# RWKV preparation: the next pair of heads projected beside the present pair's chain, no GpSimd arithmetic, reciprocal root by logarithm and exponential

## Chip, cores and metric

One NeuronCore of a Trainium2 chip runs the whole program. The metric is device time in microseconds; the kernel before takes 3918.95 us (median of three runs, 3918.48 to 3922.56). Engines are named as in the profile: PE (matrix products; PEld its weight loads), DVE, ACT, POOL, and SP, which issues DMAs.

## What is computed

Two transformer blocks, one behind the other. The change lies in the second block's RWKV-7 mixer, 8 heads of 64 channels over 1024 positions, both directions in time. In the reference's terms (T = 1024, float32):

```
u = h @ w_in; u_rwkv = u + mu_prev * (prev - u) + mu_next * (next - u)
r, k, v, g_lo, wf_lo, wb_lo, af_lo, ab_lo = split(u_rwkv)
kk = k * k_k per head; kk = kk / max(sqrt(sum(kk * kk)), 1e-12)
decay = exp(-exp(-0.5) * sigmoid(w0 + tanh(w_lo) @ w_up));  a = sigmoid(a0 + a_lo @ a_up)
k_d = k * (1 + (a_d - 1) * k_a)                    # d: forward, backward
S = S * decay - (S kk) (a kk)^T + v k_d^T;  y = S r      # scan over time, both directions
bonus = sum over head((k_f + k_b) * r * r_k) * v;  out = (groupnorm(y_f + y_b) + bonus) * g
```

Around it stand attention, output projections and a mixture of experts, which the change doesn't touch.

## The kernel before

The program is a row of stages. A stage is a block with an instruction list for each engine and its own semaphores; all engines meet at its end. Engines execute their list in order, so a wait holds up everything behind it on that engine.

Channels lie on partitions and time along the free dimension; a pair of heads is 128 channels. `stage_rwkv_low` (L1715 on) projects three blocks of 128 columns, 12 to 14 of the RWKV part: the low-rank inputs of gate, decay and rate. Each block is 48 products: 8 slices of the depth, two halves of time, and three fp32r products for one in float32 (`split_product`; `high_part` on ACT, `low_part` on DVE make the two halves of a weight, in two slots). `shifted` (L1688 on) turns a projected block into its token-shifted form: ACT copies it from PSUM with a scale (L1697), DVE adds the previous (L1701) and the next position (L1705). SP loads the weights and writes hT, the stage's input of 4 MB, to DRAM (L1740). POOL sets up `scan_reset`.

`rwkv_pairs` loops over the four pairs of heads (hardware loop `Fori`, register `pr`) with three stages:

- `stage_rwkv_prepare` (L1803 on), called the preparation below. PE projects k, r and v of this pair in float32 (L1853; a float32 product shows as two records, so a projection of 16 products is 32) and sums squares over each head (L1860). DVE and ACT turn that into the normalised key: maximum (L1925), root (L1893), reciprocal (L1927), product (L1929). Four products (L1871) make the inputs of decay and rate for both directions, ACT takes their sigmoids (L1896, L1899). DVE scans the decay within chunks of 64 positions (L1935); POOL subtracts the decay of the position itself (L1915) and multiplies rate by key (L1918); ACT takes three exponentials a direction (L1905, L1907, L1909); DVE makes the keys (L1939, L1942), the bonus' dot products (L1945, L1947, summed over heads by PE at L1877) and the four operands of the chunk stage (L1952 to L1961, `chunk_operands`).
- `stage_rwkv_chunks`: the scan in chunks of 64, some 3240 small products on PE.
- `stage_rwkv_out`: group norm, bonus and gate into `yrT[:, pr]`. SP also reads hT back, because the chunk stage's tiles overwrite it.

What is read and written where in PSUM: `bank2(n)` is two banks, 1024 columns. PE projects into `bank2` 1, 0 and 2, the norm goes to 3, decay and rate to 3, 0, 1 and 2 again. The order of the work is that of the lists and the `wait_ge` calls; nothing is planned by a program.

## Time and profile before

| | us |
|---|---|
| median of three runs | 3918.95 |
| profiled execution | 3924.63 |
| its span, first to last instruction | 3922.8 |
| low-rank stage | 46.6 |
| one pair: preparation, chunks, out | some 85, 132, 15 |
| all four pairs, 1852.9 to 2780.9 | 928 |

Engine shares of the span: PE 81%, DVE 55%, ACT 34%, POOL 11%. The profile is one execution on the chip. A row of the timeline gives the start, the duration, engine, line, operation, the tile written and the tile read, shapes and count, and in brackets how long the engine was idle before it and who ended that. PEclk is the granted clock of PE as a share of full speed: 0.5 is 1.2 GHz and 1.00 is 2.4 GHz.

### The profile page before, as it was taken

Reading aid. Unit: us, or ns where it says so; the run is one execution under the profiler, and the core shown is the slowest. Engines: PE = TensorE matmul, PEld = TensorE weight load, DVE = VectorE, ACT = ScalarE, POOL = GpSimd, SP = SyncE. Lnnn points to the kernel's source line nnn. Section 1 sums busy time; section 2 is a strip of 40 time slices with the busy share of each in tenths; the row PEclk is TensorE's granted clock in tenths of the full one; section 3 lists DMA queues with packets and bytes.
Section 4 is the critical chain, followed back from the end, with each engine's and each line's share of the span. In section 5 each row is a group of like instructions: output and inputs, shape, how many; then the busy total and the mean of one; then the engine's idle time right before and its main releaser. Section 6 shows DMA issues by size and latency. Waiting matters only on the chain. (4 is left out here: it accounts for less than half of the span.)

```text
span 3922.8 us, 58296 instructions
## 1 busy us (share of the span) xinstructions
PE 3194.4 (81%) x24517; PEld 2476.0 (63%) x24517; DVE 2172.2 (55%) x2577; ACT 1343.7 (34%) x1777; POOL 423.9 (11%) x256
## 2 busy tenths in 40 slices
PE   6699957589999898777686876769699982999995
PEld 1478745478888676654382754638466671888884
DVE  7632254456666333363674747657311238888885
ACT  1321143312121222354242423324210121777774
POOL 0200011300000010211121202112000000121210
PEclk8699977789999999898797887879799985999997
DMA  8131103111111322102001010100311224999996
GB/s 330 47 92 46 30 1 113 59 54 49 48 49 36 140 85 98 43 17 77 1 4 61 3 63 1 46 18 4 114 33 37 108 108 151 359 399 398 396 396 214
DMA packets 219994, 424.20 MB, mean 108 GB/s; under 512 B 13120, under 2 KB 122642, under 8 KB 219538
## 3 DMA queue, kind: packets, MB, share of 16 engines
q1 hardware_dynamic: 212434, 394.75, 28.1%
q0 software_dynamic: 4608, 16.78, 1.7%
q10 hardware_dynamic: 2753, 9.66, 0.6%
q8 instruction: 168, 2.75, 0.3%
q14 instruction: 31, 0.25, 0.0%
HBM read 387.61 MB, written 33.55 MB: 107 GB/s over the span
## 5 line engine op out<-in xcount | busy, mean ns | idle before, releaser
L213 DVE TENSOR_TENSOR w_exp_low<-w_exp,w_exp_high 128x2048 fp32r<-128x2048 f32 x192 | 438.0, 2291 | 56.6 <-ACT w_exp_high L208 56.5
L208 ACT ACTIVATE w_exp_high<-w_exp 128x2048 fp32r<-128x2048 f32 x192 | 367.9, 1919 | 126.2 <-PE psum L221 126.2
L219 PE MATMUL psum<-ffn_high,w_high 128*128 128x512 f32 x704 | 274.7, 390 | 9.0 <-DVE w_low L213 9.0
L220 PE MATMUL psum<-ffn_low,w_high 128*128 128x512 f32 x704 | 274.6, 390 | 0.0
L221 PE MATMUL psum<-ffn_high,w_low 128*128 128x512 f32 x704 | 274.4, 390 | 0.0
L1375 DVE SCALAR_TENSOR_TENSOR ffn_hidden<-u_padded,param_columns,ffn_hidden 128x1024 f32 (+1 forms) x176 | 226.2, 1285 | 23.8 <-DVE ffn_hidden L1375 0.2
L219 PE MATMUL psum<-w_exp_high,x_turned_high 128*128 128x512 f32 x512 | 204.0, 398 | 7.0 <-DVE w_exp_low L213 7.0
L1853 PE MATMUL psum<-mixers_hT,w_rkv 128*128 128x512 f32 x384 | 176.6, 622 | 37.7 <-DMA w_rkv<-in_w_in 37.7
L221 PE MATMUL psum<-w_exp_high,x_turned_low 128*128 128x512 f32 x512 | 201.3, 393 | 0.0
L220 PE MATMUL psum<-w_exp_low,x_turned_high 128*128 128x512 f32 x512 | 200.9, 392 | 0.0
L2288 DVE COPY inverse<-psum 64x512 f32<-64x512 f32 x192 | 121.8, 637 | 74.3 <-PE psum L2123 48.9
L1853 PEld LDWEIGHTS psum<-mixers_hT,w_rkv 128*128 128x128 f32 x384 | 76.5, 201 | 135.4 <-issue 96.1
L219 PE MATMUL psum<-ffn_down_w_split,ffn_down_lhs_split 128*128 128x512 f32 x352 | 140.4, 399 | 22.8 <-DVE ffn_down_lhs_split L213 17.2
L219 PEld LDWEIGHTS psum<-ffn_high,w_high 128*128 128x128 f32 x704 | 132.6, 188 | 36.8 <-DVE w_low L213 9.4
L2222 ACT ACTIVATE inverse<-psum 64x512 f32<-64x512 f32 x192 | 106.9, 557 | 131.7 <-PE psum L2123 105.8
L221 PEld LDWEIGHTS psum<-ffn_high,w_low 128*128 128x128 f32 x704 | 132.6, 188 | 27.6
L220 PEld LDWEIGHTS psum<-ffn_low,w_high 128*128 128x128 f32 x704 | 132.6, 188 | 27.5
L2557 DVE TENSOR_TENSOR gates_sb<-gates_sb,psum 128x1024 f32<-128x1024 f32 x16 | 19.5, 1221 | 232.7 <-PE psum L2505 232.7
L513 PE MATMUL psum<-masks,norm_h 128*128 128x128 f32 x272 | 60.2, 397 | 102.3 <-POOL norm_h L502 63.9
L213 DVE TENSOR_TENSOR ffn_down_w_split<-ffn_down_ring,ffn_down_w_split 128x1024 fp32r<-128x1024 f32 x44 | 53.9, 1225 | 158.1 <-ACT ffn_down_lhs_split L208 158.1
L220 PE MATMUL psum<-ffn_down_w_split,ffn_down_lhs_split 128*128 128x512 f32 x352 | 139.5, 396 | 0.0
L221 PE MATMUL psum<-ffn_down_w_split,ffn_down_lhs_split 128*128 128x512 f32 x352 | 139.5, 396 | 0.0
(435 smaller groups left out, 7822.3 us busy)
## 6 DMA issues: line engine op xcount, KB each, us to landing
w_exp<-in_exp_w_gate SPq DMA_DIRECT2D x32, 2048.0 KB, 11.3
w_exp<-in_exp_w_up SPq DMA_DIRECT2D x32, 2048.0 KB, 11.1
w_exp<-in_exp_w_down SPq DMA_DIRECT2D x32, 2048.0 KB, 11.4
...
```

Of the source, the lines that this page charges most:

```text
L208: return nc.scalar.activation(out, src, ACT.Copy, scale=scale)
L213: return nc.vector.tensor_tensor(out, src, high.bitcast(F32), ALU.subtract)
L219: nc.tensor.matmul(out, left[0], right[0], start=start, stop=False)
L220: nc.tensor.matmul(out, left[0], right[1], start=False, stop=False)
L221: return nc.tensor.matmul(out, left[1], right[0], start=False, stop=stop)
L513: ins = nc.tensor.transpose(ps[:, 2 * (t % 4) + k // 4, (k % 4) * P:(k % 4 + 1) * P], hbuf[:, t % SLOTS, k * P:(k + 1) * P], core.mask(M_ID))
L1375: ins = nc.vector.scalar_tensor_tensor(out=out, in0=src, scalar=weight, in1=out, op0=ALU.mult, op1=ALU.add)
L1853: ins = nc.tensor.matmul(ps[:, 2 * m + h, :], w[n][:, kt], hT[:, kt, 512 * h:512 * h + 512], start=(kt == 0), stop=(kt == KD - 1))
L2222: nc.scalar.activation(place[rows[1], :], ps[rows[1], inverse_bank(n, 1), columns], ACT.Copy).then_inc(inv_lower[n % 2], 1)
L2288: nc.vector.tensor_copy(place[rows[0], :], ps[rows[0], inverse_bank(n, 0), columns]).then_inc(inv_upper[n % 2], 1)
L2557: nc.vector.tensor_tensor(sg[:, h], sg[:, h], ps[:, 4 * h + 2:4 * h + 4, :], ALU.mult).then_inc(parts, 1)
```

## The change

- k, r and v of a pair are no longer projected in its own preparation. The first pair's are three more blocks (columns 4, 0 and 8 of 128) of the low-rank stage, six in all, with split products; the tiles `next_k`, `next_r` and `next_v` (the last quarter of `yrT`) keep them. The preparation of pair p projects those of pair p + 1 into `bank2` 1, 2 and 3 (float32 as before), if there is a next pair (`more`).
- On PE the order is now: norm, decay and rate products, projection of k and r, sums over heads for the bonus, projection of v. The shifts of all three stand at the end of ACT's and DVE's lists.
- `stage_rwkv_low`: weights in three slots used twice; the sigmoid and tanh of the low-rank inputs stand between the blocks.
- The root and reciprocal are the exponential of -0.5 times the logarithm, both on ACT.
- POOL's four operations a preparation are gone: rate by key goes to DVE; the difference and its exponential are replaced by a product of the key with the decay of the neighbouring position, a shifted read within each chunk of 64, and a copy of the key at the chunk's edge. POOL sets up `scan_reset` in each preparation, since its old place is taken.
- One exponential tile for each direction instead of one for both; v is copied out by ACT.
- The loop runs three times; the fourth pair follows as straight code without projection.

```diff
-    reset = core.reset = core.at("scan_reset", 140, [P, 2, T])
+    core.next_k = core.at("next_k_cm", 140, [P, T])
...
+    core.next_v = core.yrT[:, 3, :]
     w = [core.at(f"w_low{n}", 28 + 4 * n, [P, KD, P]) for n in range(3)]
-    split = core.at("w_low_split", 108, [P, 2, 2, KD, P], F32R)
+    split = core.at("w_low_split", 148, [P, 2, 2, KD, P], F32R)
+    blocks = [(12, low[:, 0]), (13, low[:, 1]), (14, low[:, 2]), (4, core.next_k[:]), (0, core.next_r[:]), (8, core.next_v)]
+    NB = len(blocks)
...
+        parts = [shifted(dst, flat[:, 1024 * (n % 4):1024 * (n % 4) + T], core, block, nc.scalar, nc.vector,
+                         got, half, shift, n) for n, (block, dst) in enumerate(blocks)]
...
+            for n, (block, _) in enumerate(blocks):
+                if n >= 3:
+                    sp.wait_ge(low_done, n - 2)
+                sp.dma_start(w[n % 3][:], weight_columns(dram["w_in_2"][0], block * P, P)).then_inc(w_in[n % 3], 16)
+                if n == 2:
+                    sp.dma_start(hT_in_dram(core), hT[:]).then_inc(hT_out, 16)
...
+            for n in range(NB):
                 pe.wait_ge(low_done, n + 1)
+                if n >= 4:
+                    pe.wait_ge(shift, n - 3)
...
-            for n in range(2):
-                act.wait_ge(shift, n + 1)
-                nc.scalar.activation(low[:, n], low[:, n], funcs[n]).then_inc(act_done, 1)
+                if n in (3, 4):
+                    act.wait_ge(shift, n - 2)
+                    nc.scalar.activation(low[:, n - 3], low[:, n - 3], funcs[n - 3]).then_inc(act_done, 1)
...
-            parts[0][1]()
-            take(2)
-            parts[1][1]()
-            parts[2][1]()
-
...
-        @s.b.gpsimd
-        def _(pool):
-            nc.gpsimd.memset(reset[:], 1.0).then_inc(ones_done, 1)
...
+            for n in range(NB):
+                if n + 2 < NB:
+                    take(n + 2)
+                parts[n][1]()
+
+
+def stage_rwkv_prepare(core, hT, pr, more):
...
+    k, r = core.next_k, core.next_r
+    reset = core.at("scan_reset", 44, [P, 2, T])
+    kk = core.at("kk_cm", 52, [P, T])
...
+    e = [core.at(f"growth{d}", kb, [P, T]) for d, kb in enumerate((200, 196))]
...
+    NORM, W_UP, A_UP, DOTS, NEXT = 0, (1, 2), (3, 0), 0, (1, 2, 3)
...
+        follow = ((1, k[:]), (0, r[:]), (2, core.next_v)) if more else ()
+        parts = [shifted(dst, bank2(NEXT[n]), core, pr + (4 * m + 1), nc.scalar, nc.vector, got, half, shift, n)
+                 for n, (m, dst) in enumerate(follow)]
...
+            for n, (m, _) in enumerate(follow):
+                sp.dma_start(w[n][:], weight_columns(dram["w_in_2"][0], pr * P + (m * RD + P), P)).then_inc(w_in[n], 16)
+
+        @s.b.gpsimd
+        def _(pool):
+            nc.gpsimd.memset(reset[:], 1.0).then_inc(reset_done, 1)
+            pool.wait_ge(reset_done, 1)
+            for d, first in enumerate((0, RCH - 1)):
+                nc.gpsimd.memset(chunks(reset[:, d])[:, :, first:first + 1], 0.0).then_inc(reset_done, 1)
...
+            def project(n):
...
-                        ins = nc.tensor.matmul(ps[:, 2 * m + h, :], w[n][:, kt], hT[:, kt, 512 * h:512 * h + 512],
+                        ins = nc.tensor.matmul(ps[:, 2 * NEXT[n] + h, :], w[n][:, kt], hT[:, kt, 512 * h:512 * h + 512],
...
+            pe.wait_ge(sq_done, 1)
+            over_heads(NORM).then_inc(norm_mm, 1)
...
-                ins.then_inc((w_mm, a_mm)[m], 1)
+            for d in range(2):
+                ups(0, d, W_UP[d]).then_inc(w_mm, 1)
+            ups(1, 0, A_UP[0]).then_inc(a_mm, 1)
+            pe.wait_ge(norm_cut, 1)
+            ups(1, 1, A_UP[1]).then_inc(a_mm, 1)
+            if more:
+                pe.wait_ge(sg_done, 1)
+                project(0)
+                pe.wait_ge(sg_done, 2)
+                project(1)
...
-            ins.then_inc(dots_mm, 1)
+            pe.wait_ge(a_done, 2)
+            over_heads(DOTS).then_inc(dots_mm, 1)
+            if more:
+                project(2)
...
+            nc.scalar.activation(t1[:], k[:], ACT.Square, scale=col("k_k_2")).then_inc(sq_done, 1)
+            nc.scalar.activation(vc[:], core.next_v, ACT.Copy).then_inc(v_kept, 1)
...
+            for d in range(2):
                 act.wait_ge(w_mm, d + 1)
-                nc.scalar.activation(sg[d][:], bank2(first), ACT.Sigmoid, bias=col(names["w0"][d])).then_inc(sg_done, 1)
-            for d, first in enumerate((1, 2)):
+                nc.scalar.activation(sg[d][:], bank2(W_UP[d]), ACT.Sigmoid, bias=col(("w0_f_2", "w0_b_2")[d])
+                                     ).then_inc(sg_done, 1)
+            for d in range(2):
                 act.wait_ge(a_mm, d + 1)
-                nc.scalar.activation(a[d][:], bank2(first), ACT.Sigmoid, bias=col(names["a0"][d])).then_inc(a_done, 1)
+                nc.scalar.activation(a[d][:], bank2(A_UP[d]), ACT.Sigmoid, bias=col(("a0_f_2", "a0_b_2")[d])
+                                     ).then_inc(a_done, 1)
+            act.wait_ge(norm_cut, 1)
+            nc.scalar.activation(kk[:], kk[:], ACT.Ln).then_inc(log_done, 1)
+            act.wait_ge(log_done, 1)
+            nc.scalar.activation(kk[:], kk[:], ACT.Exp, scale=-0.5).then_inc(root_done, 1)
...
             for d in range(2):
-
-                act.wait_ge(diff_done, d + 1)
-                if d:
-                    act.wait_ge(m_used, 1)
-                nc.scalar.activation(e[:], src[:, d, 0], ACT.Exp, scale=-DECAY_SCALE).then_inc(bar_exp, 1)
                 act.wait_ge(scan_done, d + 1)
                 nc.scalar.activation(src[:, d, 1], b[d][:], ACT.Exp, scale=-DECAY_SCALE).then_inc(p_exp, 1)
-                act.wait_ge(bar_used, d + 1)
-                nc.scalar.activation(e[:], b[d][:], ACT.Exp, scale=DECAY_SCALE).then_inc(m_exp, 1)
-
-        @s.b.gpsimd
-        def _(pool):
-            for d in range(2):
-                pool.wait_ge(scan_done, d + 1)
-                nc.gpsimd.tensor_tensor(src[:, d, 0], b[d][:], sg[d][:], ALU.subtract).then_inc(diff_done, 1)
-                pool.wait_ge(kk_done, 1)
-                pool.wait_ge(a_done, d + 1)
-                nc.gpsimd.tensor_tensor(src[:, d, 3], a[d][:], kk[:], ALU.mult).then_inc(akk_done, 1)
+                nc.scalar.activation(e[d][:], b[d][:], ACT.Exp, scale=DECAY_SCALE).then_inc(m_exp, 1)
+            for n in range(len(parts)):
+                act.wait_ge(rkv_mm, n + 1)
+                if n == 0:
+                    act.wait_ge(kk_done, 1)
+                    act.wait_ge(kd_done, 2)
+                if n == 1:
+                    act.wait_ge(dots_in, 1)
+                    act.wait_ge(p_used, 2)
+                if n == 2:
+                    act.wait_ge(v_kept, 1)
+                parts[n][0]()
...
 
         @s.b.vector
         def _(dve):
-            parts[0][1]()
-            parts[1][1]()
             dve.wait_ge(norm_mm, 1)
-            nc.vector.tensor_scalar(kk[:], bank2(3), 1e-24, None, ALU.max).then_inc(norm_cut, 1)
-            dve.wait_ge(norm_root, 1)
-            nc.vector.reciprocal(kk[:], kk[:]).then_inc(norm_inv, 1)
-            dve.wait_ge(norm_inv, 1)
-            nc.vector.scalar_tensor_tensor(out=kk[:], in0=k[:], scalar=col("k_k_2"), in1=kk[:], op0=ALU.mult,
-                                           op1=ALU.mult).then_inc(kk_done, 1)
-            parts[2][1]()
+            nc.vector.tensor_scalar(kk[:], bank2(NORM), 1e-24, None, ALU.max).then_inc(norm_cut, 1)
             for d in range(2):
                 dve.wait_ge(sg_done, d + 1)
                 way = slice(None) if d == 0 else slice(None, None, -1)
-                nc.vector.tensor_tensor_scan(b[d][:, way], core.reset[:, d, way], sg[d][:, way], 0.0,
+                if d == 0:
+                    dve.wait_ge(reset_done, 3)
+                nc.vector.tensor_tensor_scan(b[d][:, way], reset[:, d, way], sg[d][:, way], 0.0,
                                              ALU.mult, ALU.add).then_inc(scan_done, 1)
...
             dve.wait_ge(kd_done, 2)
+            dve.wait_ge(norm_mm, 1)
             nc.vector.tensor_tensor(t1[:], src[:, 0, 2], src[:, 1, 2], ALU.add).then_inc(sum_kd, 1)
             dve.wait_ge(sum_kd, 1)
             nc.vector.scalar_tensor_tensor(out=t1[:], in0=t1[:], scalar=col("r_k_2"), in1=r[:], op0=ALU.mult,
                                            op1=ALU.mult).then_inc(dots_in, 1)
+            dve.wait_ge(root_done, 1)
+            nc.vector.scalar_tensor_tensor(out=kk[:], in0=k[:], scalar=col("k_k_2"), in1=kk[:], op0=ALU.mult,
+                                           op1=ALU.mult).then_inc(kk_done, 1)
+            dve.wait_ge(kk_done, 1)
             for d in range(2):
-                dve.wait_ge(bar_exp, d + 1)
-                dve.wait_ge(kk_done, 1)
-                nc.vector.tensor_tensor(src[:, d, 0], kk[:], e[:], ALU.mult).then_inc(bar_used, 1)
+                nc.vector.tensor_tensor(src[:, d, 3], a[d][:], kk[:], ALU.mult).then_inc(akk_done, 1)
                 dve.wait_ge(p_exp, d + 1)
+                bar, decay, key = chunks(src[:, d, 0]), chunks(src[:, d, 1]), chunks(kk[:])
+                here, before, edge = ((slice(1, RCH), slice(0, RCH - 1), slice(0, 1)) if d == 0 else
+                                      (slice(0, RCH - 1), slice(1, RCH), slice(RCH - 1, RCH)))
+                nc.vector.tensor_tensor(bar[:, :, here], key[:, :, here], decay[:, :, before], ALU.mult)
+                nc.vector.tensor_copy(bar[:, :, edge], key[:, :, edge]).then_inc(bar_done, 1)
                 end = RCH - 1 if d == 0 else 0
-                nc.vector.tensor_copy(pl[:, d], src[:, d, 1].rearrange("p (c t) -> p c t", t=RCH)[:, :, end]
-                                      ).then_inc(pl_done, 1)
+                nc.vector.tensor_copy(pl[:, d], decay[:, :, end]).then_inc(pl_done, 1)
+                dve.wait_ge(bar_done, d + 1)
                 dve.wait_ge(pl_done, d + 1)
                 nc.vector.tensor_tensor(src[:, d, 1], src[:, d, 1], r[:], ALU.mult).then_inc(p_used, 1)
                 dve.wait_ge(m_exp, d + 1)
                 dve.wait_ge(akk_done, d + 1)
-                nc.vector.tensor_tensor(src[:, d, 2:4], src[:, d, 2:4], e.ap().unsqueeze(1).to_broadcast([P, 2, T]),
+                nc.vector.tensor_tensor(src[:, d, 2:4], src[:, d, 2:4], e[d].ap().unsqueeze(1).to_broadcast([P, 2, T]),
                                         ALU.mult).then_inc(m_used, 1)
-                if d == 0:
-                    dve.wait_ge(dots_mm, 1)
-                    nc.vector.tensor_tensor(bonus[:], bank2(0), vc[:], ALU.mult).then_inc(bonus_done, 1)
+            dve.wait_ge(v_kept, 1)
+            dve.wait_ge(dots_mm, 1)
+            nc.vector.tensor_tensor(bonus[:], bank2(DOTS), vc[:], ALU.mult).then_inc(bonus_done, 1)
+            for n in range(len(parts)):
+                parts[n][1]()
...
@@ -2430,10 +2443,13 @@
 
 
 def rwkv_pairs(core, hT):
-    with core.nc.Fori(0, RH // 2) as pr:
-        stage_rwkv_prepare(core, hT, pr)
+    with core.nc.Fori(0, RH // 2 - 1) as pr:
+        stage_rwkv_prepare(core, hT, pr, True)
         stage_rwkv_chunks(core)
         stage_rwkv_out(core, hT, pr)
+    stage_rwkv_prepare(core, hT, RH // 2 - 1, False)
+    stage_rwkv_chunks(core)
+    stage_rwkv_out(core, hT, RH // 2 - 1)
 
 
 
```

## Rows read from the trace of the kernel before

A window's row gives its stretch and length, then busy us and instructions of PE, PEld, DVE, ACT and POOL, PE's granted clock, and the DMA engines' share and GB/s.

**Rows 1.** The page's first part: engine, busy us (share of the span), instructions.
```profile
PE 3194.4 (81%) x24517; PEld 2476.0 (63%) x24517; DVE 2172.2 (55%) x2577; ACT 1343.7 (34%) x1777; POOL 423.9 (11%) x256
```

**Rows 2.** Busy time by stage: low-rank, chunks 1, preparation 2, chunks 2; columns as above.
```profile
1806.00:1852.60 46.60, 35.63 (x144) 28.94 (x144) 11.61 (x12) 9.69 (x9) 1.98 (x3) 0.89 0.35 124
...
1937.20:2069.10 131.90, 110.70 (x3240) 102.06 (x3240) 89.70 (x223) 53.32 (x121) 25.82 (x18) 0.89 0.01 3
...
2084.00:2169.50 85.50, 55.24 (x120) 23.23 (x120) 46.11 (x26) 20.92 (x19) 13.02 (x4) 0.80 0.08 21
2169.50:2301.50 132.00, 111.07 (x3240) 102.14 (x3240) 89.48 (x223) 53.26 (x121) 25.82 (x18) 0.89 0.01 3
```

**Rows 3.** Line view: first of a preparation, first of DVE in the chunk stage.
```profile
L1883 ACT ACT_TABLE_LOAD  x4: 1283/1283/1283, 1852.9 to 2549.3; - x4
...
L2275 DVE MEMSET pair_states<- x4: 165/165/165, 1937.5 to 2634.4; 128x128 f32 x4
```

**Rows 4.** Timeline, preparation of the second pair: ACT and PE.
```profile
2084.33 1.28 ACT L1883 ACT_TABLE_LOAD   x1 [3.29 <-PEq L185]
...
2089.26 30.41 PE L1853 MATMUL psum<-mixers_hT,w_rkv 128*128 128x512 f32 x64 [9.61 <-DMA w_rkv<-in_w_in]
...
2110.19 1.15 ACT L1890 ACTIVATE temp<-k_cm,param_columns 128x1024 f32<-128x1024 f32 x1 [3.00 <-DVE k_cm L1705]
...
2121.22 13.90 PE L1853 MATMUL psum<-mixers_hT,w_rkv 128*128 128x512 f32 x32
...
2135.05 3.70 PE L1871 MATMUL psum<-rwkv_low,w_ups 64*128 64x512 f32 x12
...
2138.43 2.12 ACT L1896 ACTIVATE decay_sigmoid<-psum,param_columns 128x1024 f32<-128x1024 f32 x2
...
2158.80 3.78 PE L1877 MATMUL psum<-temp,masks 128*128 128x512 f32 x4 [17.55 <-DVE temp L1947]
```

**Rows 5.** Timeline of the same preparation: DVE.
```profile
2123.76 1.22 DVE L1925 TENSOR_SCALAR kk_cm<-psum 128x1024 f32<-128x1024 f32 x1
...
2126.10 6.55 DVE L1927 RECIPROCAL kk_cm<-kk_cm 128x1024 f32<-128x1024 f32 x1 [1.12 <-ACT kk_cm L1893]
...
2139.58 4.47 DVE L1935 TENSOR_TENSOR_SCAN decay_sum<-scan_reset,decay_sigmoid 128x1024 f32<-128x1024 f32 x2 [0.36 <-ACT decay_sigmoid L1896]
...
2157.46 1.28 DVE L1947 SCALAR_TENSOR_TENSOR temp<-temp,param_columns,r_cm 128x1024 f32<-128x1024 f32 x1
...
2164.62 1.23 DVE L1952 TENSOR_TENSOR chunk_operands<-kk_cm,decay_exp 128x1024 f32<-128x1024 f32 x1
2165.76 0.17 DVE L1955 COPY pair_chunk_decay<-chunk_operands 128x16 f32<-128x16 f32 x1
...
2167.10 2.28 DVE L1961 TENSOR_TENSOR chunk_operands<-chunk_operands,decay_exp 128x2048 f32<-128x2048 f32 x1
...
2169.76 0.17 DVE L2275 MEMSET pair_states<- 128x128 f32 x1 [0.38 <-PEq L185]
```

**Rows 6.** Timeline, low-rank stage, ACT behind the first and the third block.
```profile
1826.41 1.06 ACT L208 ACTIVATE w_low_split<-w_low 128x1024 fp32r<-128x1024 f32 x1 [13.51 <-PE psum L221]
...
1848.09 1.11 ACT L1697 ACTIVATE rwkv_low<-psum,shift_keep 128x1024 f32<-128x1024 f32 x1 [9.76 <-PE psum L221]
```

**Rows 7.** Line view of L1844, the w_ups loads: from issue to landing.
```profile
DMA to landing us min/median/max: 2.5/3.4/5.6
```

**Rows 8.** Busy times of one microsecond, second pair; PEclk behind POOL's columns.
```profile
2094.00:2095.00 1.00, 1.00 (x2) 0.29 (x2) 0.00 (x0) 0.00 (x0) 0.00 (x0) 0.66 0.00 0
```

**Rows 9.** Timeline of the same preparation: POOL and DVE side by side.
```profile
2148.91 3.31 POOL L1915 TENSOR_TENSOR chunk_operands<-decay_sum,decay_sigmoid 128x1024 f32<-128x1024 f32 x1
2149.95 2.82 DVE L1939 TENSOR_SCALAR chunk_operands<-rate,param_columns,one_minus_ka 128x1024 f32<-128x1024 f32 x1
2152.19 2.78 POOL L1918 TENSOR_TENSOR chunk_operands<-rate,kk_cm 128x1024 f32<-128x1024 f32 x1
2152.81 3.24 DVE L1942 TENSOR_TENSOR chunk_operands<-chunk_operands,k_cm 128x1024 f32<-128x1024 f32 x1
```

93 lines of the change are left out of this document (29 added, 64 removed).

## Prediction, made before the change had run

> **What bounds the kernel now.** I read the page first, then the busy times by stage, then the preparation of the second pair of heads instruction by instruction. The page says that PE is busy 81% of the span [rows 1]; that is a mean over stages with different limits and says nothing of this change. The table by stage says more [rows 2]. The low-rank stage takes 46.6 us, the second pair's preparation 85.5, the chunk stage 131.9 in the first pair and 132.0 in the second. From ACT's first table load in a preparation to DVE's first instruction in the chunk stage it is 84.6 us in the first pair and 85.1 in the last [rows 3], 85.4 in the second. In a preparation PE is busy 55 of 85 us, DVE 46, ACT 21, POOL 13: no engine fills it, they take turns.
>
> The turns, in the second pair, which starts at 2084.33 [rows 4]: PE waits for weights until 2089.26, then projects k and r with the norm product behind them and v from 2121.22 on. DVE has nothing to work on but k's and r's shift and the key's norm until v is projected: the decay and rate products come at 2135.05. From there the chain is one of ACT, DVE and POOL, with PE idle but for the sums over heads at 2158.80 (3.78 us): sigmoids, scans, then DVE beside POOL, and the last product ends at 2167.10 + 2.28 = 2169.38 [rows 4, 5]. So a preparation is some 50 us of PE, then 35 us of DVE, one behind the other. The change makes them run beside each other.
>
> **1. The low-rank stage takes three more blocks.** Each is 48 split products. Blocks two and three there lie between the ACT instructions at 1826.41 and 1848.09, each of which waited for the end of a block [rows 6]: 21.68 / 2 = 10.84 us a block, 32.5 for three. The weight splitting (one ACT and one DVE instruction on 128x1024, by that shape 1.1 and 1.2 us, a block) falls into the block before, with two slots, and needs 2.5 us of 10.84. The last three weight loads are queued on SP behind the 4 MB copy of hT; the first of them is wanted two blocks after its issue (over 20 us). Nothing of this shows. The bank set that block 4 takes over was read by DVE three blocks earlier. Behind the last block, the ACT and DVE instructions of its shift take 1.11 + 2 x 1.28 as before. What ends the stage now is ACT with 1.11, a table load of 1.28 and two activations of the sigmoids' shape (2.12 for two [rows 4]), 4.5; these move forward into the blocks, 3.8 stays: 0.7 back. **Cost 31.8 us**; at worst 36 (a weight load late by half a block).
>
> **2. Pairs 1 to 3: what is left of a preparation.** I count from ACT's table load (S, 2084.33 in the second pair). Table load 1.28 and the square of k, 1.15, end at S+2.5 [rows 4]. The norm product (4 records) is the first work of PE behind an idle stretch, so it takes what the cold sum over heads took: 3.78, to S+6.4. DVE's cut of the norm: 1.22, to S+7.7 [rows 5]. The four w_ups loads are now issued first; each lands 2.5 to 5.6 us from its issue [rows 7], the last issue at about S+2.5, so PE has them at S+5.5 to S+8. Take S+6.4. The decay products of both directions run in one another's shadow (12 records took 3.70 us where one by one would be 12 x 0.43 = 5.2 [rows 4]); eight of them count as four. The clock: in the second pair PE began at 2089.26 and the granted clock rose from 0.5 (1.2 GHz) to 1.0 (2.4 GHz) within the stretch 2094 to 2095, whose mean is 0.66 [rows 8], 5.4 us later. By that it rises at S+8: two steps of 0.85, two of 0.43, decays ready at S+9.1; the rate products one step of four behind, S+10.7. The first sigmoid (2.12 for two, [rows 4]) frees the bank for the projection at S+10.3. So PE begins to project at S+10.7.
>
> From there PE is the bound: three projections of 32 records, 13.90 us each [rows 4] (0.43 a record), with the sums over heads, 4 records, now warm, 1.7: 3 x 13.8 + 1.7 = 43.1, to S+53.8. Then ACT 1.11, DVE 2 x 1.28 and some 0.2 between them for v: S+57.7, and 0.4 to the chunk stage as now (2169.38 to 2169.76): 58.1. For a later rise of the clock and the wait for w_ups I add 1.2: **59.3**. Bounds: 57 if the rise comes earlier; 63 if the norm and all the step products run at 0.85 and the first 3 us of projection too.
>
> Is DVE done by then? Scans 4.47 from S+10.4; two pairs of rate instructions (below), 4.0; sum, dot and key 3 x 1.3 [rows 5]; then, for each direction, three products of 1.23 (rate by key, the shifted decay, r), one of 2.28 and two copies of 0.17, with gaps 6.5. That is 10.4 + 4.5 + 4.0 + 3.9 + 13.0 = S+35.8. The bonus waits for the sums over heads (S+40), then k's and r's shift follow by S+47, while PE still projects v until S+54. So DVE has 7 us to spare, the reciprocal of 6.55 [rows 5] is gone from its list, and the logarithm and exponential lie on ACT, which is busy under 25 us. The memset of scan_reset on POOL, now in every preparation, has until S+10.4 for some 2 us. The gain over three pairs, 84.6, 85.4 and 85.1 less 59.3 each, is 255.1 - 177.9 = **77.2 us** (66 to 84).
>
> **3. The last pair** has no projection. DVE's list above then sets the end: S+35.8 and the bonus 1.23, with 0.4 to the next stage and 0.4 for gaps: 37.8. Gain 85.1 - 37.8 = **47.3**. One term of it is unseen: the rate instructions. They take 2.82 and 3.24 us now, but beside POOL. The second DVE product started at 2152.81, POOL's ended at 2152.19 + 2.78 = 2154.97, and DVE's ended at 2156.05: 1.08 us after POOL [rows 9]. The first, at 2149.95, ended 0.55 after POOL's 2152.22. So each seems to stand still until POOL is done, and takes 0.6 and 1.2 alone; the four then take 4.0 with gaps instead of 2 x (2.82 + 3.24) = 12.1. If the durations were their own, the last pair would be 8.1 longer (the looping pairs have 7 us of that to spare). I take the short ones.
>
> The Trainium skill (SBUF — State Buffer, § Terms) states what these rows only suggest: DVE and GpSimd arbitrate for one port pair, "Lock-allocated, exclusive, held for the full instruction". By it the four instructions fall to 4.0 us and the sum stands; by the reading in which the long durations are DVE's own the sum is -84.6. By that page the new memset on POOL, which reads no SBUF, would hold up no product of two tensors.
>
> The shifted decay is a strided read of 16 x 63 elements, which no row of this stage shows; between one and two plain products. I take the plain product's 1.23; the other end costs 2.4 in the last pair and nothing in the others.
>
> **4. The loop.** Three iterations and a straight copy. If fetching new code cost time, the first iteration's chunk stage would be longer than the second's; it is 131.9 against 132.0 [rows 2]. I cost the copy at nothing, at most 3 us. The chunk and output stages are unchanged. The chunk stage's start could profit from a PE that stopped 4 us ago rather than 7: 0 to 2 us a pair, not taken.
>
> **Sum.** -77.2 - 47.3 + 31.8 = **-92.7 us**. The profiled execution takes 3924.6 (span 3922.8), the median of the runs 3918.95; a stage's length doesn't depend on which, so I take it from the median: 3826.
>
> **Rivals.**
> A. The overlap fails. PE executes in order and the projections stand ahead of the sums over heads, and behind waits on sigmoids; if they start only when DVE's chain is done (because of a wait that I misread), a preparation is 36 + 42 + 4 = 82 us, three pairs give 3 x 3, the last 47, less 32: -24, so 3895. For it: PE's queue is one list. Against: the waits in front of the projections name sigmoids that end at S+12 and nothing later. 5%. This is also the case in which the change doesn't do what it says.
> B. The clock. In the low stretch of small products and waits PE stays at 1.2 GHz longer, and part of the projection too: 5 us more in each of three pairs, and a slow last pair, or DVE's terms at their long ends: -92.7 + 15 + 8 = -70, so 3849. The cold 3.78 of a four-record product behind an idle stretch [rows 4] speaks for it, the rise within 5.4 us against. 15%. (The Trainium skill, TensorE: Matmul & The Clock Gate, § HAM oscillation — how this bites in real kernels, warns of kernels in which waits between groups of products throw the clock back each time; in the change's first 11 us there are four such waits, each short by my sum.)
> C. Slower than before: projections at 1.2 GHz throughout. A projection took 13.90 for 32 records at the high clock; at 0.85 a record 27.2, 13.4 more, for three projections in three pairs +120, and the time is 3946. It takes that the clock doesn't rise during 40 us of PE work without a gap; the tipping point is at 77% of the records at the low clock (92.7 / 120). Against it: in the same stage now the clock rose after 5.4 us and stayed. 2%.
> D. Better than the sum: an earlier rise, a warm start of the chunk stages: -105, 3814. 14%.
>
> **Chances.** Forecast (3820 to 3836) 64%, B 15% (3836 to 3860), D 14% (3805 to 3820), A 5%, C 2%. The range 3812 to 3848 takes in the forecast, half of B and more than half of D: some 80%. A measurement of this kernel tells 0.2% (8 us) from no change. Faster by more 0.97, within 0.01, slower 0.02.
>
> **What would show it.** In the trace of after: PE's projection starts 11 us behind ACT's first table load and runs to S+54 with no wait over 1 us; the last DVE instruction of the preparation is v's second shift; the rate instructions take 0.6 and 1.2; the last preparation is 38 long and DVE fills it from S+10 on; the low stage is 78 to 79 long. It is wrong if PE waits for the sums over heads, if the granted clock is 0.5 behind S+12, or if the last pair's DVE products keep 3.2 us.

## The result, and the profile after

The changed kernel takes 3821.89 us (median of four runs, 3814.73 to 3825.96), beside 3920.76 for the kernel before on the same chip: a ratio of 0.9745, 95% interval 0.9728 to 0.9762. The forecast was 3826, between 3812 and 3848. The profiled run is the one of 3825.96; its span is 3824.1.

I divide the region that the change touches, from the first load of the low-rank stage to the merge's first load, at the first load of each stage and at DVE's memset that opens the chunk stage. Microseconds, from the two traces:

| stage | before | after | difference | forecast |
|---|---|---|---|---|
| low-rank | 47.04 | 79.15 | +32.1 | +31.8 |
| preparations 1 to 3 | 84.48, 85.31, 84.93 | 58.49, 59.35, 57.92 | -79.0 | -77.2 |
| preparation 4 | 85.00 | 34.83 | -50.2 | -47.3 |
| chunks and output, four pairs | 588.1 | 588.7 | +0.6 | 0 |
| the region | 974.9 | 878.4 | -96.5 | -92.7 |

The spans differ by 98.7, so 2.3 us lie outside the region. The first part of the page of after, as in [rows 1]:

```profile
PE 3169.6 (83%) x24565; PEld 2477.3 (65%) x24565; DVE 2125.8 (56%) x2592; ACT 1340.5 (35%) x1776; POOL 381.6 (10%) x249
```

Its busy times by stage, low-rank, preparation 2, chunks 2 and preparation 4, with the columns of [rows 2]:

```profile
1807.00:1886.20 79.20, 68.16 (x288) 55.88 (x288) 22.72 (x21) 15.90 (x15) 0.00 (x0) 0.92 0.28 93
...
2090.00:2149.50 59.50, 51.78 (x121) 22.43 (x121) 33.82 (x29) 19.32 (x18) 1.98 (x3) 0.90 0.11 29
2149.50:2281.00 131.50, 111.70 (x3240) 102.74 (x3240) 88.94 (x221) 52.94 (x120) 25.81 (x18) 0.88 0.01 3
2503.10:2538.00 34.90, 11.06 (x24) 4.13 (x24) 26.21 (x23) 15.97 (x15) 1.98 (x3) 0.60 0.01 4
```

The page alone hides the change: PE's share went from 81 to 83%, and its busy time fell by only 25 us. The second preparation shows it. PE is busy 51.8 of 59.5 us where it was 55.2 of 85.5; DVE did 33.8 us of work in those same 59.5. In the last preparation DVE is busy 26.2 of 34.9.

The timeline of the second pair's preparation, ACT and PE; it starts (S) at 2090.07 and answers to [rows 4]:

```profile
2090.07 1.28 ACT L1898 ACT_TABLE_LOAD   x1 [3.27 <-PEq L185]
...
2093.30 3.78 PE L1858 MATMUL psum<-temp,masks 128*128 128x512 f32 x4 [7.88 <-ACT temp L1899]
2097.01 4.93 PE L1865 MATMUL psum<-rwkv_low,w_ups 64*128 64x512 f32 x16
...
2100.26 2.12 ACT L1903 ACTIVATE decay_sigmoid<-psum,param_columns 128x1024 f32<-128x1024 f32 x2 [6.80 <-PE psum L1865]
...
2101.87 27.73 PE L1873 MATMUL psum<-mixers_hT,w_rkv 128*128 128x512 f32 x64
...
2104.41 1.28 ACT L1910 ACT_TABLE_LOAD   x1
...
2106.78 1.28 ACT L1912 ACT_TABLE_LOAD   x1
...
2129.44 1.88 PE L1858 MATMUL psum<-temp,masks 128*128 128x512 f32 x4
...
2131.16 13.90 PE L1873 MATMUL psum<-mixers_hT,w_rkv 128*128 128x512 f32 x32
...
2145.19 1.11 ACT L1697 ACTIVATE rwkv_out_cm<-psum,shift_keep 128x1024 f32<-128x1024 f32 x1 [14.33 <-PE psum L1873]
```

From S+11.8 on PE has no gap to S+55.0. It never waits for DVE there: the sums over heads start in the record behind k's and r's projection. DVE in the same preparation, answering to [rows 5]:

```profile
2101.41 4.47 DVE L1938 TENSOR_TENSOR_SCAN decay_sum<-scan_reset,decay_sigmoid 128x1024 f32<-128x1024 f32 x2 [3.06 <-ACT decay_sigmoid L1903]
2105.80 0.79 DVE L1942 TENSOR_SCALAR chunk_operands<-rate,param_columns,one_minus_ka 128x1024 f32<-128x1024 f32 x1
2106.62 1.23 DVE L1945 TENSOR_TENSOR chunk_operands<-chunk_operands,next_k_cm 128x1024 f32<-128x1024 f32 x1
...
2114.90 1.20 DVE L1962 TENSOR_TENSOR chunk_operands<-kk_cm,chunk_operands 128x1008 f32<-128x1008 f32 x1
...
2123.47 2.28 DVE L1971 TENSOR_TENSOR chunk_operands<-chunk_operands,growth 128x2048 f32<-128x2048 f32 x1
2131.43 1.23 DVE L1975 TENSOR_TENSOR bonus<-psum,v_cm 128x1024 f32<-128x1024 f32 x1 [5.67 <-PE psum L1858]
...
2146.45 1.28 DVE L1701 SCALAR_TENSOR_TENSOR rwkv_out_cm<-psum,param_columns,rwkv_out_cm 128x1023 f32<-128x1023 f32 x1 [8.56 <-ACT rwkv_out_cm L1697]
2147.87 1.28 DVE L1705 SCALAR_TENSOR_TENSOR rwkv_out_cm<-psum,param_columns,rwkv_out_cm 128x1023 f32<-128x1023 f32 x1
2149.53 0.17 DVE L2288 MEMSET pair_states<- 128x128 f32 x1 [0.38 <-PEq L185]
```

The brackets are DVE's idle time: 5.67 us before the bonus and 8.56 before v's shift. The chain is done at 2125.75 (S+35.7) and waits for PE. The roles have changed places: PE's list sets the end, DVE has time to spare.

### The profile page after: what moved, and what is told of

It reads as the page before. It is cut to its first block and busy times, and to the rows that moved or that the text cites. A ratio compares the mean times of both kernels' runs of the same rounds, so it can differ in the third digit from the quotient of the medians.

```text
span 3824.1 us, 58374 instructions
## 1 busy us (share of the span) xinstructions
PE 3169.6 (83%) x24565; PEld 2477.3 (65%) x24565; DVE 2125.8 (56%) x2592; ACT 1340.5 (35%) x1776; POOL 381.6 (10%) x249
## 5 line engine op out<-in xcount | busy, mean ns | idle before, releaser
L1350 ACT ACTIVATE ffn_hidden<-ffn_hidden (+1 forms) x22 | 23.3, 1061 | 295.4 <-DVE ffn_hidden L1375 295.4
L219 PE MATMUL psum<-mix_out_w_split,mix_out_lhs_split 128*128 128x512 f32 x256 | 102.8, 402 | 27.7 <-DVE mix_out_lhs_split L213 20.9
## 6 DMA issues: line engine op xcount, KB each, us to landing
w_exp<-in_exp_w_up SPq DMA_DIRECT2D x32, 2048.0 KB, 10.4
```

The source lines that it names most:

```text
L219: nc.tensor.matmul(out, left[0], right[0], start=start, stop=False)
L1350: nc.scalar.activation(block(i * 2 + (j - 1)), block(i * 2 + (j - 1)), ACT.Silu).then_inc(silu_done, 1)
```

## Experiments

Whole times of one kernel lie within 11 us (after: 3814.73 to 3825.96), so a part worth less than 10 us is read from its stage, with the divisions of the table above. A "preparation" below is always such a length. It scatters too, by about 1 us, but only in its first part: from the projection's start to the chunk stage it is 47.66 us in each of the three looping preparations of after (2149.53 less 2101.87 in the second), and from the scans' start to the chunk stage 25.73 in the last (2538.11 less 2512.38). An edit behind these two points can be read from those lengths to a few hundredths. Diffs are against the changed kernel unless the text says otherwise, and are excerpts.

### The first half of the overlap taken away

```diff
-            if more:
-                pe.wait_ge(sg_done, 1)
-                project(0)
-                pe.wait_ge(sg_done, 2)
-                project(1)
...
-                project(2)
+                for n in range(3):
+                    project(n)
```

All three projections stand behind the sums over heads; everything else is as changed. DVE's list behind the dot products (the key, the operands, the bonus, 14 us) still runs beside them, so this takes away the overlap of the chain's first half only.

> The changed kernel, with all three projections of the next pair moved behind the sums over heads in PE's list, so behind DVE's dot products; the number of instructions is the same. Theory (the gain of pairs 1 to 3 is the overlap of PE's projections with the chain on ACT and DVE): in the changed kernel the dot products end 22.5 us behind a preparation's start and PE started to project at 11.8; now it idles, runs the sums over heads at the low clock (3.8), and starts to project at about 26, the first 5 us at the low clock. The preparation of pairs 1 to 3 grows from 59.5 to 74 or 75 us, the last pair's stays at 34.9, the whole is 45 us longer than the changed kernel. Rival (the gain comes from the shorter chain, and PE's order hardly matters): the preparation grows by less than 5 us.

Measured: 3862.01 us (3857.13 to 3870.72, four runs), ratio to before 0.9845 (0.9829 to 0.9861). Preparations 71.15, 72.41, 72.14 and 35.18; low-rank stage 79.26. PE in the second pair's preparation:

```profile
2132.62 3.78 PE L1858 MATMUL psum<-temp,masks 128*128 128x512 f32 x4 [10.64 <-DVE temp L1946]
2136.20 41.47 PE L1873 MATMUL psum<-mixers_hT,w_rkv 128*128 128x512 f32 x96
```

PE waits 10.64 us for DVE, takes 3.78 instead of 1.88 for the sums over heads, and then the three projections in one stretch. That costs 12.7 to 14.2 us in each of the first three preparations (39.9 in sum) and nothing in the last. So the order on PE is worth some 13 us a pair, and the last preparation's gain doesn't hang on it: there no projection is left at all. It is less than the 14.5 to 15.5 us a pair, 45 in all, that I expected: I had put the projection's first 5 us at the low clock, but the clock rose 3.8 us behind the start of the sums over heads, at about 2136.4, and 96 records took 41.47 us, 0.43 each.

### The chain alone

The kernel before, with its projections where they were, but the new chain: logarithm and exponential, the shifted product, rate by key on DVE, two exponential tiles, no POOL. (Diff against the kernel before, excerpts.)

```diff
-                    nc.scalar.activation(kk[:], kk[:], ACT.Sqrt).then_inc(norm_root, 1)
+                    nc.scalar.activation(kk[:], kk[:], ACT.Ln).then_inc(norm_root, 1)
+                    act.wait_ge(norm_root, 1)
+                    nc.scalar.activation(kk[:], kk[:], ACT.Exp, scale=-0.5).then_inc(norm_inv, 1)
...
-                nc.gpsimd.tensor_tensor(src[:, d, 0], b[d][:], sg[d][:], ALU.subtract).then_inc(diff_done, 1)
...
-            nc.vector.reciprocal(kk[:], kk[:]).then_inc(norm_inv, 1)
...
+                nc.vector.tensor_tensor(bar[:, :, here], key[:, :, here], decay[:, :, before], ALU.mult)
+                nc.vector.tensor_copy(bar[:, :, edge], key[:, :, edge]).then_inc(bar_used, 1)
```

> The kernel before, with only the edits of the chain: logarithm and exponential for root and reciprocal, rate by key on DVE, the shifted product in place of POOL's difference and its exponential. The projections stay where they were, the loop runs four times. Theory (what counts is the chain behind the projection of v, and the reciprocal was hidden behind that projection): DVE's list from the first scan to the last product took 29.8 us in the kernel before and 25.4 in the changed kernel's last pair, of which the key's product, 1.2, is done earlier here: 5.6 us less in each of four preparations, 22 us in all. Rival (each DVE instruction that goes is worth its own time): the reciprocal's 6.55 on top, 12 us a preparation and 48 in all.

Measured: 3898.69 us (3893.88 to 3902.68), ratio 0.9939 (0.9922 to 0.9955). Preparations 78.98, 79.37, 79.03, 79.14: 5.5, 5.9, 5.9 and 5.9 less than before. From PE and DVE of the second pair:

```profile
2119.70 13.90 PE L1854 MATMUL psum<-mixers_hT,w_rkv 128*128 128x512 f32 x32
...
2127.06 1.28 DVE L1915 SCALAR_TENSOR_TENSOR kk_cm<-k_cm,param_columns,kk_cm 128x1024 f32<-128x1024 f32 x1 [3.60 <-ACT kk_cm L1896]
...
2138.06 4.47 DVE L1921 TENSOR_TENSOR_SCAN decay_sum<-scan_reset,decay_sigmoid 128x1024 f32<-128x1024 f32 x2 [0.36 <-ACT decay_sigmoid L1899]
```

The key is ready at 2128.34, while v is projected until 2133.60 and the scans start only at 2138.06. The reciprocal of 6.55 us [rows 5] lay in that shadow before, so taking it away gains nothing here; the 5.8 come from the chain behind the scans.

### The old chain beside the overlap, whole and by one part

First the reciprocal alone (root, then DVE's reciprocal), then with it POOL's four operations and the exponential of the difference.

```diff
-            nc.scalar.activation(kk[:], kk[:], ACT.Ln).then_inc(log_done, 1)
-            act.wait_ge(log_done, 1)
-            nc.scalar.activation(kk[:], kk[:], ACT.Exp, scale=-0.5).then_inc(root_done, 1)
+            nc.scalar.activation(kk[:], kk[:], ACT.Sqrt).then_inc(root_done, 1)
...
+            nc.vector.reciprocal(kk[:], kk[:]).then_inc(log_done, 1)
+            dve.wait_ge(log_done, 1)
```

> The changed kernel with one part of the old chain: root on ACT and reciprocal on DVE instead of logarithm and exponential. Theory (as for the old chain): 6.5 us more in the last preparation, nothing in the first three, 6.5 in all. Rival (DVE sets the end everywhere): 26 us.

Measured: 3828.53 us (3820.82 to 3831.94), ratio 0.9767 (0.975 to 0.9783). Preparations 57.79, 59.9, 58.35 and 41.65: nothing in the first three beyond their scatter, 6.8 in the last. From the projection's start it is 47.66 in all three, as in after; from the last preparation's scans 32.33, 6.6 more. DVE has the 6.55 us to spare beside a projection and not without one.

The whole old chain adds to this (the two exponential tiles of the changed kernel stay):

```diff
+                nc.gpsimd.tensor_tensor(src[:, d, 0], b[d][:], sg[d][:], ALU.subtract).then_inc(diff_done, 1)
...
+                nc.gpsimd.tensor_tensor(src[:, d, 3], a[d][:], kk[:], ALU.mult).then_inc(akk_done, 1)
...
+                nc.scalar.activation(src[:, d, 0], src[:, d, 0], ACT.Exp, scale=-DECAY_SCALE).then_inc(bar_exp, 1)
...
-                nc.vector.tensor_tensor(src[:, d, 3], a[d][:], kk[:], ALU.mult).then_inc(akk_done, 1)
+                nc.vector.tensor_tensor(src[:, d, 0], src[:, d, 0], kk[:], ALU.mult).then_inc(bar_done, 1)
```

> The changed kernel with the old chain: root on ACT and reciprocal on DVE, and POOL's difference and rate by key back, with the difference's exponential on ACT. The projections stay beside the chain. Theory (PE sets the end in pairs 1 to 3, where DVE has 5.7 us idle ahead of the bonus and 8.6 ahead of v's shift; DVE sets it in the last pair): the last preparation grows by 6.6 for the reciprocal and by up to 10.4 for the stretches in which DVE stands still beside POOL, from 34.9 to 47 to 52; the first three by 0 to 3 each; 12 to 26 us in all. Rival (DVE's chain still sets the end in all four): 50 us or more.

Measured: 3841.84 us (3832.81 to 3846.28), ratio 0.9802 (0.9785 to 0.9818). Preparations 58.59, 58.34, 57.95 and 47.40: the last is 12.6 longer, the others are not; from the projection's start they are 47.66 or 47.67 again. POOL and DVE in the last one:

```profile
2507.30 7.00 POOL L1855 TENSOR_TENSOR chunk_operands<-decay_sum,decay_sigmoid 128x1024 f32<-128x1024 f32 x2 [9.32 <-DVE decay_sum L1945]
2509.32 2.77 DVE L1949 TENSOR_SCALAR chunk_operands<-rate,param_columns,one_minus_ka 128x1024 f32<-128x1024 f32 x1
2512.13 3.26 DVE L1952 TENSOR_TENSOR chunk_operands<-chunk_operands,next_k_cm 128x1024 f32<-128x1024 f32 x1
2515.31 0.80 DVE L1949 TENSOR_SCALAR chunk_operands<-rate,param_columns,one_minus_ka 128x1024 f32<-128x1024 f32 x1
2516.15 1.23 DVE L1952 TENSOR_TENSOR chunk_operands<-chunk_operands,next_k_cm 128x1024 f32<-128x1024 f32 x1
...
2527.82 5.67 POOL L1859 TENSOR_TENSOR chunk_operands<-rate,kk_cm 128x1024 f32<-128x1024 f32 x2 [13.51 <-DVE kk_cm L1962]
2528.91 2.31 DVE L1971 COPY pair_chunk_decay<-chunk_operands 128x16 f32<-128x16 f32 x1
```

The same two DVE instructions take 2.77 and 3.26 us beside POOL, and 0.80 and 1.23 once POOL has ended at 2514.30. Even the copy of 16 columns, 0.17 us elsewhere, takes 2.31. So of the chain's 23.2 us in the kernel before, 12.6 are left once PE sets the end of three preparations: the parts' gains overlap each other (the chain alone took 25.3 off the region, the overlap with the old chain 85.5, both 96.5).

### POOL's work put back without its dependences

These two settle whether the long durations come from POOL's being busy or from its reading SBUF. POOL works on the reset tile, which nobody needs any more, once the scans are done. First two products:

```diff
+            pool.wait_ge(scan_done, 2)
+            nc.gpsimd.tensor_tensor(reset[:, 0], reset[:, 0], reset[:, 1], ALU.mult).then_inc(reset_done, 1)
+            pool.wait_ge(reset_done, 4)
+            nc.gpsimd.tensor_tensor(reset[:, 0], reset[:, 0], reset[:, 1], ALU.mult).then_inc(reset_done, 1)
```

> The changed kernel with two POOL instructions that nobody waits for: products of two SBUF tensors of 128x1024, started when the second scan is done, as the first rate instruction is. Theory (a DVE instruction of this chain stands still while a POOL product runs; in the kernel before each ended 0.55 or 1.08 us behind POOL's): of the four rate instructions, 0.8 and 1.2 us long in the changed kernel, those beside POOL grow to the end of POOL's, 2 to 3.3 us; together 4 to 7 us more, in the last preparation at full size (35 becomes 39 to 42), in the others hidden in DVE's idle time. Rival (the 2.8 and 3.2 us of the kernel before were DVE's own, from the operands' places): the four keep 0.8 and 1.2.

Measured (one run, 3821.26): the last preparation 39.56 us, 4.7 longer, of which 4.1 lie behind the scans' start; the others 58.56, 59.39, 58.81. The last preparation:

```profile
2506.97 0.79 DVE L1946 TENSOR_SCALAR chunk_operands<-rate,param_columns,one_minus_ka 128x1024 f32<-128x1024 f32 x1
2507.13 2.83 POOL L1854 TENSOR_TENSOR scan_reset<-scan_reset 128x1024 f32<-128x1024 f32 x1 [11.96 <-DVE decay_sum L1942]
2507.79 3.25 DVE L1949 TENSOR_TENSOR chunk_operands<-chunk_operands,next_k_cm 128x1024 f32<-128x1024 f32 x1
2510.03 3.22 POOL L1856 TENSOR_TENSOR scan_reset<-scan_reset 128x1024 f32<-128x1024 f32 x1
2510.97 2.85 DVE L1946 TENSOR_SCALAR chunk_operands<-rate,param_columns,one_minus_ka 128x1024 f32<-128x1024 f32 x1
```

No data passes between the two engines, yet each DVE instruction that starts while POOL works ends 0.57 to 1.08 us after POOL (2511.04 against 2509.96, 2513.82 against 2513.25). Then three memsets of the same tile in the products' place:

```diff
+            nc.gpsimd.memset(reset[:], 1.0).then_inc(reset_done, 1)
```

> The same with three POOL memsets of 128x2048 (1.8 us each) in place of the products: they write SBUF and read nothing. Theory of one lock for every POOL instruction: rate instructions grow as beside the products, by up to 4 us in all. Rival (only a POOL instruction that reads SBUF holds up DVE's product of two tensors, while the single-tensor rate instruction may still be held up): the product keeps 1.2 us, the single-tensor one grows by up to 1.8.

Measured (one run, 3820.19): the last preparation 35.55, of which 26.04 lie behind the scans' start, 0.3 more than in after; the others 58.43, 59.12, 58.70.

```profile
2511.01 2.39 POOL L1854 MEMSET scan_reset<- 128x2048 f32 x1 [11.70 <-DVE decay_sum L1944]
2511.70 1.23 DVE L1951 TENSOR_TENSOR chunk_operands<-chunk_operands,next_k_cm 128x1024 f32<-128x1024 f32 x1
2512.84 1.11 DVE L1948 TENSOR_SCALAR chunk_operands<-rate,param_columns,one_minus_ka 128x1024 f32<-128x1024 f32 x1
2513.46 2.23 POOL L1856 MEMSET scan_reset<- 128x2048 f32 x1
...
2515.75 1.81 POOL L1858 MEMSET scan_reset<- 128x2048 f32 x1
```

The rival came out. The product of two tensors keeps its 1.23 beside a memset, and waits for a POOL product. The rate instruction that reads one tensor and columns is held up by both, here from 0.81 to 1.11, and it holds the memset up in turn: the two memsets that start while one runs take 2.39 and 2.23, the third, which meets only products of two tensors, 1.81. That a product of two tensors is held up only by a POOL instruction that reads SBUF is what the prediction took from the Trainium skill, SBUF — State Buffer (§ Terms, and § SBUF: two separate sides), and these two runs agree with it. For the sizes there is one run of each; the second and the last preparation of it agree.

### Where the first 11 us go

From S (in this and the next two sections SP's first load, 0.1 us behind ACT's first instruction in the second pair) to the projection nothing of PE's is hidden. Three edits shorten the ends of a looping preparation. The first moves the sigmoid's table load from the start of the preparation to the end of ACT's list in the stage before:

```diff
-            nc.scalar.preload_act_table(ACT.Sigmoid)
...
+            nc.scalar.preload_act_table(ACT.Sigmoid)
```

> The changed kernel with the sigmoid's table loaded at the end of ACT's list in the output stage, where ACT idles, rather than ahead of k's square. Theory (from a preparation's start to the norm product ACT is the path: table load 1.28, square 1.15): the norm product starts 1.9 rather than 3.2 us behind the start, and each of four preparations is 1.3 us shorter, 5 in all. Rival (the small w_ups loads take the place of the wait; by issue and landing they are there 5.0 to 5.6 us behind the start): the decay products start where they did, and the gain is under 0.5 us each.

Measured (one run, 3825.84): preparations 56.32, 59.47, 59.43, 34.60. The first is 2.2 shorter, the second and third are not, though ACT's square stands at the start of each. The square and the norm product, first and third pair:

```profile
1888.82 1.15 ACT L1898 ACTIVATE temp<-next_k_cm,param_columns 128x1024 f32<-128x1024 f32 x1 [3.16 <-PEq L185]
...
1890.02 3.78 PE L1858 MATMUL psum<-temp,masks 128*128 128x512 f32 x4 [5.51 <-ACT temp L1898]
...
2298.05 1.15 ACT L1898 ACTIVATE temp<-next_k_cm,param_columns 128x1024 f32<-128x1024 f32 x1 [2.07 <-PEq L185]
...
2301.65 3.78 PE L1858 MATMUL psum<-temp,masks 128*128 128x512 f32 x4 [8.37 <-issue]
```

In the first pair PE starts 1.20 us behind the square's start. In the third it starts 3.60 behind, 2.45 after the square has ended, and the trace names no engine that it waited for ("issue"). These are the preparations that are entered by the loop's jump back, and in them an instruction packet is moved:

```profile
q8 instruction: 1, 0.02, 0.9%
```

That is the DMA view from 2292 to 2302. PE seems to wait for its own instructions; the test is below. The last preparation isn't entered by the jump and its norm product does start 1.3 us earlier (S+1.2 for S+2.5), yet it is only 0.2 us shorter than after's: its granted clock rose at S+6.5, after's at S+5.6. In the first, 2.2 us shorter for a norm product 1.2 us earlier, the clock rose at S+5.0 instead of S+8.1.

The second edit shifts v in two halves, the first while PE projects the second:

```diff
+                    if n == 2 and h == 0:
+                        ins.then_inc(v_half, 1)
...
+                    for h, ready in enumerate(((v_half, 1), (rkv_mm, 3))):
+                        act.wait_ge(*ready)
+                        cols = slice(512 * h, 512 * h + 512)
+                        nc.scalar.activation(core.next_v[:, cols], bank2(NEXT[2])[:, cols], ACT.Copy,
+                                             scale=core.keep[:, bass.ds(pr + 9, 1)]).then_inc(got, 1)
...
```

> The changed kernel with the shift of v, last in pairs 1 to 3, taken in two halves of time, the first while PE projects the second half. Theory (behind PE's last product come ACT 1.11 and DVE 2 x 1.28 in full, 4.0 us): half the columns need 0.7 + 2 x 0.7 = 2.1, so 1.7 to 1.9 less in each of three preparations, 5 us in all; the last preparation is unchanged. Rival (PE's end isn't what the tail hangs on): no change.

Measured (one run, 3822.61): preparations 56.79, 56.11, 57.49, 35.22. The first three sum to 170.39, beside 175.76 in after: 5.4 less, with nothing in the last. In the second pair the chunk stage opens 2.67 us after v's last product instead of 4.47. Single preparations moved by 0.4 to 3.2, but from the projection's start each of the three is 45.86 us long instead of 47.66: 1.80 less each, as in the theory. The rest of the moves lies ahead of the projection.

### The changed kernel again, and one table for both functions

The changed kernel once more, as the measure for the next runs on that chip:

> The changed kernel itself, unedited, for its time on the chip on which the two below run. Expected: 97 us below the kernel before, from the stages of its first profile (low-rank +32, preparations -126, the rest even); both theories of the runs below take it as their zero.

Measured: 3823.62 us (3816.56 to 3830.47, five runs), ratio 0.9746 (0.9732 to 0.976); preparations 58.49, 59.20, 59.10, 35.78. A preparation repeats within 1.2 us. The next kernel names the set that holds logarithm and exponential:

```diff
+            nc.scalar.preload_act_table_set("natural_log_exp_and_others")
```

> The changed kernel with one table set that holds logarithm and exponential, loaded once, in place of two loads. Theory (ACT is not on the path there; in the last pair the exponential of the norm ended 3.2 us ahead of its use): one load of 1.28 us less on ACT in each preparation, all stages as long as before, within 0.3 us. Rival (ACT's exponentials set when DVE's products start): 1.3 us less in the last preparation.

Measured (one run, 3827.49): preparations 58.54, 59.48, 58.77, 35.18. ACT in the second:

```profile
2108.06 1.28 ACT L1909 ACT_TABLE_LOAD   x1
2109.35 1.06 ACT L1911 ACTIVATE kk_cm<-kk_cm 128x1024 f32<-128x1024 f32 x1
2110.44 1.06 ACT L1913 ACTIVATE kk_cm<-kk_cm 128x1024 f32<-128x1024 f32 x1
```

One load of 1.28 us has gone, and no stage is shorter by it: from the projection's start the first three are 47.66 or 47.67 as in after, and from the scans' start the last is 25.75, where it is 25.73 in after and 25.75 in its repetition. ACT isn't what ends any of them. (The Trainium skill, ScalarE: Activation LUTs, § Table sets: the hidden batching unit, has a logarithm and an exponential behind it share one load. In the trace of after they take two, L1910 and L1912; only with the set named is it one.)

### All three, and then no loop

> The changed kernel with the table load moved to the output stage, v's shift in halves, and one table set for logarithm and exponential. Theory (the parts lie one behind the other on the path of pairs 1 to 3): 3.1 us less in each of three preparations, 1.3 in the last, 10.5 us less than the changed kernel. Rival (one gives back what the other gains, at the w_ups loads or at DVE): 5 us or less.

Measured: 3810.17 us (3807.56 to 3817.3, five runs), ratio 0.971 (0.9697 to 0.9724). Preparations 54.47, 56.16, 57.64, 34.90, together 7.4 less than after and 9.4 less than its repetition. The halves of v's shift give their 1.80 in each of the first three (45.86 from the projection's start). It is short of the expected 10.5 where the table load's 1.3 us fails again: the norm product starts at S+3.1 in pairs 2 and 3, and at S+1.2 in pairs 1 and 4; and the fourth, at 34.90, isn't shorter than in after, since its clock rose 1.5 us later.

If PE waits there for instructions behind the jump, straight code takes the wait away:

```diff
-    with core.nc.Fori(0, RH // 2 - 1) as pr:
-        stage_rwkv_prepare(core, hT, pr, True)
+    for pr in range(RH // 2):
+        stage_rwkv_prepare(core, hT, pr, pr < RH // 2 - 1)
...
```

> The kernel with all three edits, with the four pairs written out as straight code instead of a hardware loop of three and a copy. With the table load moved, k's square ended 1.2 us behind a preparation's start in every pair, but PE's norm product stood at 1.2 only in pairs 1 and 4, and at 3.1 to 3.6 in pairs 2 and 3, which are entered by the loop's jump; a 16 KB instruction packet lies in the microsecond behind that start, and none in pair 4's. Theory (PE waits for its instructions behind the jump): in straight code the norm product starts at 1.2 in all four, preparations 2 and 3 are 2 us shorter, 4 us in all and no stage longer. Rival (it is the second and third pair's data, or the reload of hT): it stays at 3.1 to 3.6. Second rival (straight code is fetched more slowly): chunk stages longer than 132 us.

Measured: 3807.59 us (3802.22 to 3815.89, five runs), ratio 0.9709 (0.9696 to 0.9723). Preparations 54.59, 55.33, 54.63, 34.61. The second pair's norm product:

```profile
2080.83 1.15 ACT L1900 ACTIVATE temp<-next_k_cm,param_columns 128x1024 f32<-128x1024 f32 x1 [1.51 <-PEq L185]
...
2082.03 3.78 PE L1858 MATMUL psum<-temp,masks 128*128 128x512 f32 x4 [5.26 <-ACT temp L1900]
```

Its releaser is ACT again, at S+1.23, as in all four pairs, and no instruction packet is moved from 2072 to 2082. In both looping pairs it starts 1.9 us earlier than with the loop, which is what the theory said; the rival is out, and the second rival too, since chunk and output stages are 583.8 us together for 584.1. The second and third preparations are 3.8 us shorter together, and that this is 2 x 1.9 is partly luck: the second is 0.8 shorter and the third 3.0. One-microsecond rows, third pair, with the loop and without; PE's clock is the third number from the end:

```profile
2297.22:2298.22 1.00, 1.00 (x6) 0.36 (x6) 0.00 (x0) 0.00 (x0) 0.00 (x0) 0.84 0.82 197
...
2288.59:2289.59 1.00, 1.00 (x5) 0.53 (x6) 0.95 (x1) 0.00 (x0) 0.00 (x0) 0.91 1.15 345
```

By them PE's clock rose there at S+9.3 with the loop and at S+5.2 without; in the second pair it rose at S+6.3 and S+6.6. So an earlier norm product is shown, and what a stage gains by it depends on when the clock rises. The whole times of the last two kernels can't be told apart. Both beat the kernel before and the changed one: the region is 861.88 us long, beside 974.89 and 878.44.

## Why the prediction came out right

**The low-rank stage** was forecast at +31.8 and is +32.1. Blocks that differ only in their columns cost what their neighbours cost.

**Preparations 1 to 3.** Offsets from S in the second pair, forecast and measured:

| step | forecast | measured |
|---|---|---|
| norm product ends | 6.4 | 7.0 |
| scans start | 10.4 | 11.3 |
| projection starts | 10.7 | 11.8 |
| DVE's chain done | 35.8 | 35.7 |
| bonus starts | 40 | 41.4 |
| v projected | 53.8 | 55.0 |
| chunk stage | 58.1 + 1.2 | 59.5 |

The scans and the projection start a microsecond late, and PE's steps behind them keep their distance; DVE's chain took 24.3 us instead of 25.4 and made its delay good. In this pair the allowance of 1.2 for a later rise of the clock was needed: one-microsecond rows of this stretch, with PE's clock behind POOL's columns, have a clock of 0.85 between 2099 and 2100, so it rose at about 2099.3, 6.0 us from PE's start at 2093.30, where [rows 8] had it after 5.4. Over the three pairs most of it was not: the projection starts at S+10.8, 11.7 and 10.3 (from SP's first load) and the stages are 58.5, 59.35 and 57.9, on average 0.5 us above the sum of 58.1. That unused allowance is nearly all of the 1.8 us between -77.2 and -79.0.

```profile
2098.00:2099.00 1.00, 1.00 (x6) 0.47 (x4) 0.34 (x1) 0.00 (x0) 0.00 (x0) 0.50 1.14 329
2099.00:2100.00 1.00, 1.00 (x8) 0.46 (x5) 0.00 (x0) 0.00 (x0) 0.00 (x0) 0.85 1.16 300
```

The wait for w_ups, the other half of that allowance, was no wait: the product with them follows the norm product at once. As the stage's first issues they landed in 2.0 to 3.0 us, not 2.5 to 5.6 [rows 7]. In its place stood a delay that I hadn't listed, the norm product's late start after the jump back: the square ends at S+2.5, the product starts at S+3.2 (S+3.1 from SP's first load).

**The last preparation** was the least exact step: 34.8 for 37.8. Its three terms are all too long, by 1.3, 1.2 and 0.5. The scans start at S+9.1 instead of 10.4, since the clock rose 3.2 us after PE's start. From there to DVE's last product with the growth it is 24.2 us instead of 25.4, because instructions in a row start before the sum of their durations is reached (in the second pair 2106.62 + 1.23 is 2107.85, and the next starts at 2107.76) and I had put gaps between them. The bonus and the step to the chunk stage take 1.5, not 2.0.

**The unseen rows.** The rate instructions alone take 0.79 and 1.23, forecast 0.6 and 1.2 against 2.82 and 3.24 [rows 9]; the shifted decay takes 1.20, forecast 1.23 against twice that. For the rate instructions I had taken what each had left behind POOL's end, for the shifted decay a plain product's time, and both choices carried: had the rate instructions kept their times, the last preparation would be 8 us longer. The four took 4.0 us as forecast, by two errors that cancel: 0.8 where I had 0.6, and no gaps. POOL's products put back show the cause directly.

**The rivals.** A, that the overlap fails, is ruled out by PE's unbroken stretch from S+11.8 to S+55.0; no run makes it fail whole. The run that starts the projections behind the dot products, at S+26 and not behind all of DVE's chain, loses 13 us a pair and ends at 72, not at A's 82. B, a clock that stays low, did not happen: the projection runs at 0.43 us a record from its first, 27.73 for 64. C falls with it. D, better than the sum, holds in one part: the third and the last preparation had an earlier rise. Chunk stages did not gain: with their output stages they are 588.7 us together where they were 588.1.

**The loop** was costed at nothing, at most 3 us. The fourth preparation, a copy, pays nothing. In the iterations entered by the jump back the norm product starts at S+3.1 (3.1 to 3.7 in the other runs with the table load in its place) where the first and fourth have it at S+2.4 and S+2.5, both from SP's first load; with the table load away it is 3.1 to 3.6 against 1.2. So in the changed kernel PE starts some 0.7 to 1.2 us late in two preparations, and by more once ACT is faster. In the kernel before nothing of this could show, since PE waited for weights until S+4.9 [rows 4].
